# Second phase of a hybrid recurrent decoder step: one dense quantum per block moves from behind the HGRN levels to in front of the Mamba squares' sum

## The reference, cut to what matters

```python
mod = c_act @ P['w_ada'][l] + P['b_ada'][l]
h = rmsnorm(x, P['g_norm1'][l]) * (1.0 + sc1) + sh1
mix, states = token_mix(h, ...)          # HGRN2 | Mamba-2 | RWKV-7, then @ w_out
x = x + (g1 * mix)
h = rmsnorm(x, P['g_norm2'][l]) * (1.0 + sc2) + sh2
ff = (silu(h @ w_gate) * (h @ w_up)) @ w_down
x = x + (g2 * ff)
...
o_hg = rmsnorm(o_hg, g) * silu(hg_g)     # HGRN2 heads
y_mb = (y_mb + D * m_x) * silu(mb_z)     # Mamba-2 output
y_mb = rmsnorm(y_mb, g)                  # sum of squares over 256 channels
```

## Time and profile before

| | us |
|---|---|
| median of 3 runs | 1803.08 |
| lowest, highest | 1802.68, 1806.28 |
| profiled execution | 1808.78 |
| its span, first to last instruction | 1807.1 |
| PE busy in it | 1590.2 (88%) |
| DVE, ACT, POOL busy | 1042.7, 660.4, 251.8 |

### The profile page before, as it was taken

One profiled execution on the slowest core, in us unless ns is written; L12 is line 12 of the kernel. 1 busy time (PEld: TensorE's weight loads), 2 busy tenths in 40 slices (PEclk: granted clock), 3 DMA queues, 4 the chain that ended last, 5 costly groups with the idle time before them and its releaser, 6 DMA issues.

```text
span 1807.1 us, 32642 instructions
## 1 busy us (share of the span) xinstructions
PE 1590.2 (88%) x13639; PEld 1452.5 (80%) x13639; DVE 1042.7 (58%) x2152; ACT 660.4 (37%) x1133; POOL 251.8 (14%) x331
## 2 busy tenths in 40 slices
PE   4799999879998677696888899999899999999997
PEld 2798888768787433484777799998899999999997
DVE  5514455767564555776765344576665556665554
ACT  3323333223332422343433253343444444533333
POOL 4411111111111210231334400100000000000000
PEclk9899999879999677697988999999999999999999
DMA  8111001011111254321121444534464535554552
GB/s 317 53 47 36 25 25 36 32 40 46 40 59 45 102 191 147 103 80 41 51 83 53 138 125 133 148 121 125 131 188 143 161 117 154 150 174 133 148 147 78
DMA packets 276683, 188.09 MB, mean 104 GB/s; under 512 B 7879, under 2 KB 264376, under 8 KB 275512
## 3 DMA queue, kind: packets, MB, share of 16 engines
q1 hardware_dynamic: 266050, 160.28, 29.6%
q0 software_dynamic: 7536, 22.47, 3.8%
q10 hardware_dynamic: 2950, 3.24, 0.5%
HBM read 172.82 MB, written 13.18 MB: 103 GB/s over the span
## 4 chain that ended last, share of the span: by engine, by line
PE 69%; DVE 17%; ACT 7%; issue 4%; DMA 1%; SPq 0%; POOL 0%; DVEq 0%; ACTq 0%; POOLq 0%
PE bank L1344 18%; PE bank L1345 17%; PE bank L1346 17%; PE bank L1280 3%; ACT WHI L1949 2%; DVE WLO L2432 1%; PE bank L1517 1%; PE bank L1510 1%; PE bank L1519 1%; PE bank L1687 1%; PE bank L1366 1%; PE bank L1454 1%; DMA ADAW<-in_w_ada 1%; DVE ACC L2452 1%; PE bank L1375 1%
## 5 line engine op out<-in xcount | busy, mean ns | idle before, releaser
L2432 DVE TENSOR_TENSOR WLO<-RAW,WHI 128x1024 fp32r<-128x1024 f32 (+4 forms) x235 | 247.2, 1052 | 266.5 <-ACT WHI L1949 264.8
L1949 ACT CAST WHI<-RAW 128x1024 fp32r<-128x1024 f32 (+4 forms) x294 | 266.2, 909 | 227.7 <-PE bank L1346 198.7
L1344 PE MATMUL bank<-HAH,WHI 128*128 128x384 f32 (+1 forms) x832 | 277.9, 334 | 12.1 <-DVE HAL L2615 6.6
L1345 PE MATMUL bank<-HAL,WHI 128*128 128x384 f32 (+1 forms) x832 | 274.0, 329 | 0.0
L1346 PE MATMUL bank<-HAH,WLO 128*128 128x384 f32 (+1 forms) x832 | 273.5, 329 | 0.0
L1344 PE MATMUL bank<-HHI,WHI 128*128 128x344 f32 x568 | 191.2, 337 | 10.1 <-DVE HLO L2651 5.9
L1091 POOL TENSOR_TENSOR WLO<-RAW,WHI 128x1024 fp32r<-128x1024 f32 (+1 forms) x59 | 127.2, 2159 | 438.7 <-ACT WHI L1949 438.6
L1345 PE MATMUL bank<-HLO,WHI 128*128 128x344 f32 x568 | 185.1, 326 | 0.0
L1346 PE MATMUL bank<-HHI,WLO 128*128 128x344 f32 x568 | 184.9, 326 | 0.0
L1344 PE MATMUL bank<-MIXR,WHI 128*128 128x384 f32 (+2 forms) x528 | 173.7, 329 | 12.4 <-DVE MIXR L2562 3.8
L1344 PEld LDWEIGHTS bank<-HAH,WHI 128*128 128x128 f32 x832 | 160.4, 193 | 16.0 <-issue 15.3
(11 more groups left out here) (582 smaller groups left out, 2778.8 us busy)
## 6 DMA issues: line engine op xcount, KB each, us to landing
RAW<-in_w_gate SPq DMA_DIRECT2D x66, 512.0 KB, 3.9
RAW<-in_w_up SPq DMA_DIRECT2D x66, 512.0 KB, 4.0
RAW<-in_w_ada SPq DMA_DIRECT2D x32, 512.0 KB, 4.3
RAW<-in_w_in SPq DMA_DIRECT2D x26, 512.0 KB, 3.8
RAW<-in_w_out SPq DMA_DIRECT2D x24, 512.0 KB, 3.6
RAW<-in_w_down SPq DMA_DIRECT2D x32, 384.0 KB, 3.2
RAW<-in_w_down SPq DMA_DIRECT2D x32, 320.0 KB, 2.9
ADAW<-in_w_ada SPq DMA_DIRECT2D x8, 1024.0 KB, 19.9
```

Of the source, the lines that this page charges most:

```text
L1344: mm(bank[:, 0:w], whi[:, k, :], hi_k, start=(k == 0), stop=False)
L1345: mm(bank[:, 0:w], whi[:, k, :], lo_k, start=False, stop=False)
L1949: a.copy(w_split(i)[0][:, 0:nk, :], RAW[u % NRAW][:, 0:nk, :]).then_inc(w_hi, 1)
L2432: v.tensor_tensor(wlo[:, 0:nk, :], RAW[u % NRAW][:, 0:nk, :], whi[:, 0:nk, :].bitcast(F32), ALU.subtract).then_inc(w_lo, 1)
```

## The change

Two numbers of the table change: after `mb_turn` stand four halves of quanta instead of two, and after `hg_levels` none instead of two.

```diff
-        FILL = {'hg_att': 2, 'mb_decay': 2, 'hg_o': 2, 'mb_prod': 2, 'mb_turn': 2, 'hg_levels': 2}
+        FILL = {'hg_att': 2, 'mb_decay': 2, 'hg_o': 2, 'mb_prod': 2, 'mb_turn': 4, 'hg_levels': 0}
```

## The result

The changed kernel took 1811.14 us (median of 15 runs, 1803.57 to 1818.06), the kernel before 1802.51 us in as many runs beside it: ratio 1.0041, 95% interval 1.0024 to 1.0057. It is slower by 7.4 us, where 4.2 us were forecast. Its profiled execution took 1818.06 us.

What follows compares the result with a forecast made beforehand. PE was taken to bound the kernel, its stops reaching the end whole. Starts of -1.3 us plus clock costs of +5.45 gave +4.2 us, 1807.3 us on the median; range 1800.5 to 1811.5.

Steps and rivals of the forecast that it cites:

- The two stops become one: At each of the four places, PE's two stops merge into one of about the same length; no gain of any size.
- the clock behind `hg_att`: Behind `hg_att` in block 3 the clock falls to the low level too: 5.4 us at half speed, costing 2.7 us.
- the forecast's own case: One exposed chain per block and PE colder behind it: +2 to +7 us; chance 0.55, of which 0.42 beyond +3.6.
- The clock inside `hg_att`: Low clock inside `hg_att`: 0.55 us for each first half in blocks 4 to 6, 1.1 for both halves in block 3.
- The net starts: Shift of the quantum behind `hg_att`: +0.7, +0.5, +0.4 and -2.9 us in blocks 3 to 6, together -1.3.
- The sum at the low clock in block 4: In block 4 the forecast took 2.12 us from the sum's start to RM's end.
- The fourth rival: Clearly slower: POOL also holds evictions, sums start at the low clock (0.9 us each); +8 to +10 us, chance 0.10.
- The middle in block 6: In block 6 the chain was taken to end midway between 953.4 and 955.8, moving the next quantum's start by -2.9 us.
- the later bound: In block 6 two low parts on POOL hold up DVE's products, so the levels end at 955.8.
- ACT is free by then, so the second stop goes away: In `hg_att`, PE's wait for ACT's copy of H0 (7.7 us in four waits) disappears; `hg_att` takes 2.54 us.
- The even exchange: Rival: POOL waits for DVE in block 6, clock falls no more often than before; -1.4 to +2 us, chance 0.25.
- The faster case: Rival: block 6 decides, levels undisturbed there and in block 3, nearly no clock cost; -4 to -5 us, chance 0.10.

Runs made afterwards that it cites:

- The shift: The changed kernel with 32 small matmuls that nobody reads added on PE ahead of the squares' sum of block 2: 1815.7 us, ratio 1.0082.
- POOL's low part later: The changed kernel with POOL starting the low part of the tile cast behind quantum B only after the levels, blocks 3 to 6: 1806.68 us, ratio 1.0014.
- the kernel with added matmuls: The changed kernel with unread 128 by 128 matmuls added in PE's stops before and behind the sums of blocks 3 to 6: 1811.0 us, ratio 1.0039.

## Why the prediction was right or wrong

**Right: the sign, the mechanism in the main, and which wait ends where.** "The two stops become one" came out as told. The idle before the sums was forecast at 2.1, 3.3, 4.6 and 3.3 us and is 2.14, 3.25, 4.55 and 3.24; the second stop is released by RM in block 4 and by the levels in blocks 3 and 5; no wait for H0's copy is left; the clock behind `hg_att` of block 3 is 0.51, and the quantum there is 2.44 us longer, where 2.7 were forecast. The time, 1811.1 on a forecast of 1807.3, lies just inside the upper edge of the range, 1811.5, and the measured +7.4 us outside the +2 to +7 of the forecast's own case.

**Wrong: the size.** Against +4.2 us stand +8.0 in place; four terms were too small, one of them not there at all, and one was missing on the other side. That the latter gave 2.1 us back helped the time into the range, and nothing in the prediction had foreseen it.

- *The clock inside `hg_att`* (the step "in blocks 4 to 6 the second half was slow before; now the first is slow as well, 3 x 0.55"). The net starts had been worked out with an `hg_att` at full clock, 2.54 us, and compared with a before whose second half was slow. Both halves had to be added on that side, 3 x 1.1. This is an error of my working, 1.65 us, and the traces bear it out: without its stops `hg_att` took 3.1, 3.0 and 3.0 us in blocks 4 to 6 before and 3.7 in block 5 after. In block 5, which has no other surprise, the start moved by +1.33 against a mended +1.5.
- *The sum at the low clock in block 4.* The 2.12 us from the sum's start to RM's end came from a sum of 1.16 us. Here it took 2.08, and where RM decides that is 0.92 more. The fourth rival held this term; the forecast did not. In blocks 3, 5 and 6 the levels end last and it costs nothing.
- *The middle in block 6.* I took the middle between 953.4 and 955.8 for the end of the chain. The levels ended 965.50 - 949.39 = 16.1 us after A's start; the middle would have been 15.35 and the later bound 16.55, so I was 0.8 short. Both low parts held DVE's products, for 2.79 and 2.43 us, and the low part of 4.80 us on which I had leaned did not repeat in this order. By the rule of the Trainium skill, "SBUF — State Buffer", section "Who interferes with whom", that the instruction issued first keeps the port for its whole length, the prediction had found the later bound. By those two rows the trace agrees with it here. Holding POOL back gave 1.18 us of the stop back in block 6.
- *Not in the prediction at all: the instruction stream*, 1.36 us in block 4 and 1.70 us in block 6. Before, packets fell into the waits for H0's copy in these two blocks. What failed is the step "ACT is free by then, so the second stop goes away": the stop went, and what it had covered came out.
- *The clock behind `hg_att`, the other way.* In blocks 4 to 6 the low level had begun ahead of `hg_att` and ended earlier in the quantum: the granted clock over the whole quantum was 0.65, 0.80 and 0.73 where it had been 0.60, 0.68 and 0.61, and the quantum was 0.4, 0.8 and 0.9 us shorter. The prediction had left these three at zero.

Block by block, with the mended terms: 1.8 - 0.5 (the levels ended 15.5 us after A's start, not 16.0) = 1.3, measured 1.42; 1.05 + 0.55 + 0.92 + 1.36 = 3.88, measured 3.80; 0.95 + 0.55 = 1.5, measured 1.33; -2.3 + 0.55 + 0.8 + 1.70 = 0.75, measured 1.09.

**The rivals.** The even exchange needed block 6 to gain 4 us; it lost 1.1. The faster case named block 6 as the place that decides, and needed the levels undisturbed there and the clock at full; the changed kernel had neither. With T left early and POOL held, the same order on PE is worth 0.6%, so this rival's mechanism exists, but it takes two edits that the change does not make. The fourth rival, +8 to +10, was nearer than its chance of 0.10: the sums did run at the low level in the profiled execution and POOL did hold products in block 6, but the sums cost only in block 4, and it had nothing of the instruction stream either.

**Open.** In place the changed kernel loses 8.0 us, to the end 6.9; where 1.1 us comes back later was not looked for. The shift shows that the packets set where the gaps are, and what a gap costs in its place; that the kernel as a whole would win the 3.1 us without them is only argued, since no run has the changed order on all engines without them. What makes the clock fall at one place in one execution and not in the next is not shown either. The sum of block 3 took 2.00 us in the changed kernel and 1.16 in two others with the same order on PE in that block (POOL's low part later, and the shifted stream).

## What to carry to other kernels

When a work item is moved in an order that all engines share, cost it engine by engine: here the same move is worth +0.4% made on all of them, -0.2% or so made on PE alone, and -0.6% where POOL makes way as well, because the chain to be covered must keep its early place on the engines that feed it. When a stop goes away, ask what else ran to its end beneath it, DMAs of the instruction stream among them. And compare like with like: a start worked out at full clock may only be set against a row at full clock.

## What the runs showed of the hardware that I had not expected

- A dense run of small matmuls outruns the loading of its own instructions. PE's stream comes in 16 KB packets of 0.9 to 1.5 us on its own queue, and PE went on 1.24 to 1.55 us after a packet's end in 25 of 25 gaps. A gap put into a block cost 1.9 and 2.7 us, one taken out gave 2.2. `hg_att` (transposes, 192 matmuls of 64 by 32 and their weight loads) took 2.49 us at full clock where no packet stopped it; in block 4 it took 5.39 us begun at full clock and 5.31 at the low level.
- A low clock level behind `hg_att` came with such a gap and without one. In the kernel with added matmuls the transposes in block 4 took 0.41 us and the first dense matmul behind the gap 0.69; in block 3, which had no gap, they took 0.44 and 0.69. Keeping TensorE busy ahead of the small matmuls did not keep the clock up behind them.
- Two low parts of POOL back to back (4.71 us) held VectorE for 2.8 us over two products and for 2.4 us over one, which take 0.6 and 0.28 us alone.
